# PEER experts on 192 tokens densely and on the last 64 by their chosen rows

## The chip, the cores and the metric

The kernel runs on one core of a Trainium2 chip. The metric is the device time of one execution in microseconds (us): 3215.98 us, the median of three runs (3214.02 to 3218.95). The profile below is of one execution of the same program, with a span of 3216.2 us from its first to its last instruction.

## The reference

Two transformer blocks act on 256 tokens of width 2048, all in float32. What matters here is the last part of the first block, a "PEER" layer with 16384 experts:

```python
def peer(h, w_q, sub_keys, expert_u, expert_v):        # T = 256 tokens, D = 2048
    q = (xt @ w_q).reshape(T, 8, 2, 128)
    s = jnp.einsum('thpd,hpnd->thpn', q, sub_keys)     # 8 heads x 2 halves x 128 keys
    s_half, i_half = lax.top_k(s, 16)
    ...                                                # best 16 of the 16 x 16 pairs of each head
    g = jax.nn.softmax(top_s, axis=-1)                 # 8 x 16 = 128 chosen experts for a token
    u = expert_u[ic]                                   # expert_u, expert_v: 16384 x 2048
    a = jnp.einsum('cd,ced->ce', xc, u)
    w = gc * jax.nn.gelu(a)
    return jnp.einsum('ce,ced->cd', w, expert_v[ic])
```

Each token needs 128 of the 16384 rows of `expert_u` and of `expert_v`. The first block's attention comes before it; the second block (`w_in_2`, two branches, `w_out_2`, and a feed-forward with `w_up` and `w_down`) comes after it.

## The kernel before

**Weights in pieces.** All big weights are cut on the host into pieces of 128 x 1024 float32 (512 KB). The list `order` fixes the order of its 1104 pieces: among them 32 of `peer_w_q`, 256 of `peer_u`, 256 of `peer_v`, then 160 of `w_in_2`. SyncE loads piece after piece into `raw` (`NR` = 5 buffers). ScalarE rounds it to fp32r (`split_hi`, into `whi`, `NH` = 3 buffers), VectorE subtracts to get the remainder (`split_lo`, into `wlo`), and TensorE multiplies high part by high, high by low and low by high. That makes two kinds of products:

- `gemm` (`peer_v`, `w_in_2`, `w_down`): the activations are the stationary operand, the weights move, 12 matmuls of 512 columns for a piece (`gemm_piece`).
- `gemm_wide` (`peer_w_q`, `peer_u`, `w_up`): the weights are stationary; high and low activations of 256 tokens stand side by side and move together, so a piece takes 8 matmuls of 512 columns with `whi` and 8 of 256 columns with `wlo` (`wide_piece`). Four pieces make one unit of 256 output rows.

**The PEER layer is dense.** `peer_u` is multiplied with all tokens (64 units of 256 experts). `u_post` adds the two halves of the result on VectorE (`gelu_sum`, 128 x 512), scales it (`gelu_scale`), takes the gelu on ScalarE and stores it to `scr_a`. Meanwhile `routing` finds each token's 128 experts on VectorE, and GpSimd writes their gates into a zeroed table `scr_g` of 16384 x 256 in DRAM with 256 indirect DMAs (`gate_scatter`, 128 elements of 4 bytes each, L2913). `fetch` reads gelu and gate back, `prepare` multiplies them and splits the product, and `peer_v` is multiplied with it. `add_residual` adds each of its products to `R`.

**What sets the order.** The whole program is recorded by one walk of Python generators (`walk`); `tasks` holds those that run beside the products, and `step()` moves each of them to its next `yield`. `gemm_wide` calls `step()` after three of a unit's four pieces, and more steps are taken where it must have a result. So a generator's number of yields fixes beside which piece each of its instructions stands. Every engine then runs its own list in that order and waits on semaphores: a VectorE instruction that waits for a DMA holds up the `split_lo` behind it. `scatter` issues four indirect DMAs for each `yield`.

## Time and profile before

| | |
|---|---|
| runs | 3214.02, 3215.98, 3218.95 us |
| span of the profiled execution | 3216.2 us |
| TensorE busy | 3182.5 us, 99% |
| VectorE busy | 2082.1 us, 65% |
| ScalarE busy | 1523.1 us, 47% |
| GpSimd busy | 531.3 us, 17% |
| moved by DMA | 663.12 MB, mean 206 GB/s |

The span is the time to compare with a run; no time around it is listed. "Idle before" in a group is the time in which the engine stood still just before these instructions, with what it waited for. A stretch's DMA share is the mean busy share of the core's 16 DMA engines. A matmul's shown duration overlaps the next one's, so a matmul's cost is read from the distance of starts.

### The profile page before, as it was taken

The page shows a single profiled execution, that of the slowest core. Times are in us where ns is not written, and L with a number is a line of the kernel's source. Part 1 is how long each engine was busy: PE and PEld are TensorE (multiplying, and loading weights), DVE is VectorE, ACT ScalarE, POOL GpSimd, SP SyncE. Part 2 cuts the span into 40 slices and gives each one's busy share as a digit, 9 for nine tenths or more (in the row PEclk, how much of TensorE's full clock was granted, in tenths as well). Part 3 has the DMA queues.
Part 4 walks back from the last instruction along what each step waited for, and adds up shares of the span by engine and source line. Part 5 has one row for each costly group of instructions (what it writes and reads, how often), then busy time and mean ns, then how long its engine had stood idle before and what let it go on. Part 6 is the DMA issues. An engine that isn't in the chain of part 4 may idle for free.

```text
span 3216.2 us, 41890 instructions
## 1 busy us (share of the span) xinstructions
PE 3182.5 (99%) x16120; PEld 2701.5 (84%) x16120; DVE 2082.1 (65%) x3024; ACT 1523.1 (47%) x2006; POOL 531.3 (17%) x326
## 2 busy tenths in 40 slices
PE   9899999999999999999999999999999999999998
PEld 7788888888888888888888888888888888888886
DVE  6786588886555576666666665555465755555556
ACT  5655454454444444444444544455444544444443
POOL 0010007788777400000000000000000000000000
PEclk9999999999999999999999999999999999999999
DMA  7466558888888876677776555455655655666654
GB/s 260 138 231 240 185 206 208 211 215 216 213 208 213 266 278 232 235 241 248 247 244 195 189 189 176 163 171 171 202 198 175 198 193 186 195 190 190 191 192 147
DMA packets 220599, 663.12 MB, mean 206 GB/s; under 512 B 56896, under 2 KB 56912, under 8 KB 217584
## 3 DMA queue, kind: packets, MB, share of 16 engines
q1 hardware_dynamic: 170784, 600.81, 56.8%
q0 software_dynamic: 49472, 59.59, 8.8%
q8 instruction: 127, 2.08, 0.3%
q14 instruction: 72, 0.59, 0.1%
q10 hardware_dynamic: 144, 0.05, 0.0%
HBM read 624.57 MB, written 35.78 MB: 205 GB/s over the span
## 4 chain that ended last, share of the span: by engine, by line
PE 96%; DVE 2%; ACT 1%; issue 1%; DMA 0%; SPq 0%; DVEq 0%; ACTq 0%
PE PS L1785 94%; PE PS L1880 1%; DVE wlo L2285 0%; ACT whi L2041 0%; DMA raw<-in_w_in_a 0%; DVE AA L2339 0%; ACT M L2015 0%; DVE Y L2451 0%; ACT Y L2141 0%; DVE R L2814 0%; DVE BB L2339 0%; DVE M L2481 0%; DVE RT L2269 0%; DVE Y L2532 0%; DVE M L2391 0%
## 5 line engine op out<-in xcount | busy, mean ns | idle before, releaser
L2285 DVE TENSOR_TENSOR wlo<-raw,whi 128x1024 fp32r<-128x1024 f32 x1101 | 1342.5, 1223 | 737.3 <-ACT whi L2041 727.5
L2041 ACT ACTIVATE whi<-raw 128x1024 fp32r<-128x1024 f32 x1101 | 1159.9, 1058 | 1012.1 <-PE PS L1785 983.0
L1785 PE MATMUL PS<-whi,AA 128*128 128x512 f32 x2816 | 703.6, 391 | 3.4 <-DVE AA L2339 1.8
L1785 PE MATMUL PS<-whi,BB 128*128 128x512 f32 x2640 | 666.7, 393 | 1.7 <-DVE wlo L2285 1.2
L1785 PEld LDWEIGHTS PS<-whi,AA 128*128 128x128 f32 x2816 | 525.1, 188 | 113.3 <-DVE AA L2339 2.2
L1785 PE MATMUL PS<-BB,whi 128*128 128x512 f32 x2304 | 577.4, 392 | 0.5 <-DVE BB L2339 0.5
L1785 PEld LDWEIGHTS PS<-whi,BB 128*128 128x128 f32 x2640 | 491.3, 188 | 102.2 <-DVE wlo L2285 1.6
L2913 POOL DMA_INDIRECT scr_g<-M x256 | 480.1, 1875 | 352.0 <-DVE M L2687 224.5
L1785 PEld LDWEIGHTS PS<-BB,whi 128*128 128x128 f32 x2304 | 414.4, 189 | 74.9 <-DVE BB L2339 0.8
L1785 PE MATMUL PS<-wlo,AA 128*128 128x512 f32 x1408 | 379.1, 389 | 0.0
L1785 PE MATMUL PS<-wlo,BB 128*128 128x512 f32 x1320 | 356.4, 390 | 0.5 <-DVE wlo L2285 0.5
L1785 PEld LDWEIGHTS PS<-BB,wlo 128*128 128x128 f32 x2304 | 314.3, 190 | 22.5
L1785 PE MATMUL PS<-BB,wlo 128*128 128x256 f32 x2304 | 321.2, 282 | 0.0
L1785 PEld LDWEIGHTS PS<-wlo,AA 128*128 128x128 f32 x1408 | 264.3, 188 | 55.5
L1785 PEld LDWEIGHTS PS<-wlo,BB 128*128 128x128 f32 x1320 | 247.7, 188 | 53.1 <-DVE wlo L2285 0.9
L1785 PE MATMUL PS<-AA,whi 128*128 128x512 f32 (+1 forms) x1056 | 262.1, 389 | 1.8 <-DVE AA L2380 1.1
L1785 PEld LDWEIGHTS PS<-AA,whi 128*128 128x128 f32 (+1 forms) x1056 | 188.5, 187 | 35.6 <-DVE AA L2380 1.4
L1785 PEld LDWEIGHTS PS<-AA,wlo 128*128 128x128 f32 (+1 forms) x1040 | 141.7, 189 | 10.3 <-DVE wlo L2285 0.4
L1785 PE MATMUL PS<-AA,wlo 128*128 128x256 f32 (+1 forms) x1040 | 147.3, 282 | 0.0
L2580 DVE TENSOR_TENSOR R<-R,PS 128x512 f32<-128x512 f32 x128 | 82.2, 684 | 77.1 <-PE PS L1785 77.1
L2941 POOL TENSOR_TENSOR R<-R,M 128x512 f32<-128x512 f32 x4 | 5.9, 1489 | 707.7 <-ACT M L2015 707.7
L2015 ACT ACTIVATE M<-TMP 128x512 f32<-128x512 f32 x64 | 40.5, 632 | 152.1 <-DVE TMP L2706 137.1
(252 smaller groups left out, 1520.5 us busy)
## 6 DMA issues: line engine op xcount, KB each, us to landing
raw<-in_peer_u SPq DMA_DIRECT2D x256, 512.0 KB
raw<-in_peer_v SPq DMA_DIRECT2D x256, 512.0 KB
raw<-in_w_in SPq DMA_DIRECT2D x160, 512.0 KB
raw<-in_w_up SPq DMA_DIRECT2D x128, 512.0 KB
raw<-in_w_down SPq DMA_DIRECT2D x128, 512.0 KB
raw<-in_w_out SPq DMA_DIRECT2D x64, 512.0 KB
raw<-in_w_in_a SPq DMA_DIRECT2D x32, 512.0 KB
scr_g<-M POOLq DMA_DIRECT2D x8, 2048.0 KB, 32.5
```

The lines of the kernel that those rows point to most:

```text
L1785: return e.matmul(outp, l, r, start=start, stop=stop)
L1880: last = e.transpose(banks[bank][:, 128 * n:128 * n + 128], s, ident)
L2015: e.activation(o, x, func, **kw).then_inc(sem(name), 1)
L2041: e.activation(whi[:, n % NH, :], raw[:, n % NR, :], ACT.Copy).then_inc(s_hi, 1)
L2285: e.tensor_tensor(wlo[:, n % NH, :], raw[:, n % NR, :], bf(whi[:, n % NH, :]), ALU.subtract).then_inc(s_lo, 1)
L2580: last = e.tensor_tensor(R[:, t, c], R[:, t, c], b[t][:, :], ALU.add)
L2913: e.indirect_dma_start(out=D["scr_g"].rearrange("e (t o) -> (e t) o", o=1), out_offset=bass.IndirectOffsetOnAxis(ap=EID[t][:, k:k + 1], ax ...
L2941: e.tensor_tensor(R[:, t, c], R[:, t, c], scaled[j], ALU.add).then_inc(sem("pool_added"), 1)
```

## The change

The constant `NSP` = 64 parts the tokens: the first `TD` = 192 keep the dense form, the last 64 get their experts by rows.

- Dense part: `peer_u` runs with `T=TD`, so a piece takes 8 matmuls of 384 columns and 8 of 192. `peer_v` is cut as `peer_u` is and uses `gemm_wide` with `T=TD` in place of `gemm`; its result comes out transposed and is added to `YT`, a transposed copy of the rows, which is turned back at the end. The two activation buffers `AA` and `BB` change roles from there on.
- The table `scr_g` has 192 columns; the 128 scatters of the second token tile write 64 elements each. `scatter` issues 1.5 for each `yield`, the second tile is routed first, and `fetch` and `prepare` work by 256 experts instead of 1024.
- Sparse part: 128 partitions hold 64 tokens twice, and each of the two copies takes 64 of a token's 128 experts. For each m in 0..63 GpSimd gathers 128 rows of `peer_u` (8 KB each, 1 MB in all, L3177) and VectorE multiplies and sums them with the token's row (`sparse_dot`, two halves of 1024). After the gelu and the gate, for each m GpSimd gathers 128 rows of `peer_v` (L3184), and VectorE adds them weighted (`sparse_add`, two halves). A matmul with the constant `select` sums the two copies.
- At u = 59 the recording takes steps with no product between them until the last dot is recorded.

The core of the diff:

```diff
+NSP = 64
+TD = 256 - NSP
...
+    SCATTERS, DOT_PACE, ADD_PACE = 1.5, ((1, 1), (1, 0)), (1, 1)
...
                     for k in range(16):
+                        while credit < 1.0:
+                            yield
+                            credit += SCATTERS
+                        credit -= 1.0
                         go("gate_scatter", t, 16 * h + k, fresh("POOL", ready, landed[t] if k == 0 else None))
                         mark = landing(f"gate_scattered{t}")
-                        if k % 4 == 3:
-                            yield
...
-                    for t in range(2):
+                    for t in (1, 0):
...
+            def sparse_dots():
+                dots, rows_free = {}, {}
+                for m in range(NSP + 2):
+                    if m < NSP:
+                        while not t_z:
+                            yield
+                        go("gather_u", m, fresh("POOL", sp_routed[0], sp_routed[1], t_z, rows_free.get(m - 3)))
+                        dots[m] = landing(f"rows_landed{m % 3}")
+                    for half in range(2):
+                        for _ in range(DOT_PACE[m % 2][half]):
+                            yield
+                        if m >= 2:
+                            go("sparse_dot", m - 2, half, fresh("DVE", dots[m - 2], t_z))
+                            last = up("DVE", "sparse_step")
+                    if m >= 2:
+                        rows_free[m - 2] = last
...
             for u in range(64):
-                gemm_wide("peer_u", [u], BB, nP, u_post)
+                gemm_wide("peer_u", [u], BB, nP, u_post, T=TD)
...
+                if u == 59:
+                    while not sp_weighed or len(g_written) < 2:
+                        step()
+                    assert not idle
+                    for n in range(4):
+                        fetch(n)
+                if u == 61:
+                    tasks.append(prepare())
...
+            def sparse_adds():
+                rows_in, rows_free = {}, {}
+                for m in range(NSP + 1):
+                    if m < NSP:
+                        go("gather_v", m, fresh("POOL", sp_weighed, bar, g_written, rows_free.get(m - 2)))
+                        rows_in[m] = landing(f"rows_landed{m % 2}")
+                    for half in range(2):
+                        for _ in range(ADD_PACE[half]):
+                            yield
+                        if m >= 1:
+                            go("sparse_add", m - 1, half, fresh("DVE", rows_in[m - 1], sp_weighed, bar, latest["DVE"]))
+                            last = up("DVE", "sparse_step")
...
+            for c in range(8):
...
+                for db in range(8):
+                    gemm_wide("peer_v", [8 * c + db], HB[c % 2], wB[c], v_post, T=TD)
...
-                    x = both[:, kt, :, :].rearrange("p a n -> p (a n)")
+                    x = both[:, kt, :, 0:T]
...
-                        last = mm(b[m][:, 0:256], wlo[:, s, w], both[:, kt, 0, :], False, kt == 15)
+                        last = mm(b[m][:, 0:T], wlo[:, s, w], both[:, kt, 0, 0:T], False, kt == 15)
...
+            def sparse_dot(m, half, ready):
...
+                e.tensor_tensor_reduce(out=x, in0=x, in1=z_all[:, c], scale=1.0, scalar=0.0, op0=ALU.mult, op1=ALU.add,
+                                       accum_out=sp_dot[:, half, m:m + 1]).then_inc(sem("sparse_step"), 1)
...
+                    last = e.scalar_tensor_tensor(out=v_sum[:, c], in0=x, scalar=sp_w[:, m:m + 1], in1=v_sum[:, c],
+                                                  op0=ALU.mult, op1=ALU.add)
...
+                n = (128, P0)[t]
                 e.indirect_dma_start(out=D["scr_g"].rearrange("e (t o) -> (e t) o", o=1),
...
+            def gather_u(m, ready):
...
+                e.indirect_dma_start(out=u_rows[m % 3], out_offset=None, in_=D["peer_u_rows"],
+                                     in_offset=bass.IndirectOffsetOnAxis(ap=sp_id[:, m:m + 1], axis=0)
+                                     ).then_inc(sem(f"rows_landed{m % 3}"), 16)
```

How it moves the instructions, at three places.

**GpSimd, from the routing's end to the first fetch.** Before, the last scatters stand alone (L2913), and the fetches follow (L2922 gelu, L2923 gates):

```order
L2913 DMA scr_g<-M 4194304x1 [waits gate_scattered1]
L2913 DMA scr_g<-M 4194304x1 x15
L2922 DMA M<-scr_a 128x2048 [waits gelu_stored2,gelu_stored1,gelu_stored3,gelu_stored0,gate_scattered0,gelu,gate_scattered1,piece_used,gelu_scaled]
L2923 DMA M<-scr_g 128x8x256
L2922 DMA M<-scr_a 128x2048 [waits gelu_stored2,gelu_stored3,gelu_stored1,gelu_stored0]
L2923 DMA M<-scr_g 128x8x256
```

Now, after 112 of the 256 scatters (L3150), the second norm's gain (L3158), the tokens' rows (L3164) and then the gathers of `peer_u` (L3177) stand between them:

```order
L3158 DMA M<-in_gain 64x2048 [waits gelu,piece_used,gelu_scaled]
L3150 DMA scr_g<-M 3145728x1 [waits gate_scattered0]
L3150 DMA scr_g<-M 3145728x1 x7
L3164 DMA M<-M 64x2048 [waits sparse_step]
L3164 DMA M<-M 64x2048
L3177 DMA M<-in_peer_u_rows,PTb 128x2048 [waits z_landed,routes_landed1,routes_landed0]
L3150 DMA scr_g<-M 3145728x1 x3
L3177 DMA M<-in_peer_u_rows,PTb 128x2048
L3150 DMA scr_g<-M 3145728x1
L3177 DMA M<-in_peer_u_rows,PTb 128x2048
L3150 DMA scr_g<-M 3145728x1 x3
L3177 DMA M<-in_peer_u_rows,PTb 128x2048 [waits sparse_step]
```

From the first gather on, 136 scatters and 64 gathers share this engine's list, about two scatters for a gather; before, nothing stood between two scatters.

**VectorE, beside `peer_u`.** Before, behind the routing (its last instruction is the CAST), an added half (L2700) and a scaling (L2706) stand between the splits (L2285) of every four pieces:

```order
L2687 CAST M<-M 128x64 [waits vector_step]
L2285 TENSOR_TENSOR wlo<-raw,whi 128x1024 [waits piece_used,hi_split]
L2706 TENSOR_TENSOR TMP<-TMP,PTb 128x512 [waits gelu_sum]
L2285 TENSOR_TENSOR wlo<-raw,whi 128x1024 [waits piece_used,hi_split] x2
L2700 TENSOR_TENSOR TMP<-TMP,PS 128x512 [waits gelu_low]
L2285 TENSOR_TENSOR wlo<-raw,whi 128x1024 [waits piece_used,hi_split] x2
```

Now dots (L2911, each with a read of its sum, `PTb 128x1`) stand there too, four for every four pieces, each second one behind a gather's `rows_landed`; here where the last dots begin:

```order
L2911 ISA M,PTb<-M 128x1024 [waits rows_landed2]
L2911 ISA PTb 128x1
L2464 TENSOR_TENSOR wlo<-raw,whi 128x1024 [waits piece_used,hi_split]
L2879 TENSOR_TENSOR TMP<-TMP,PS 128x384 [waits gelu_low]
L2911 ISA M,PTb<-M 128x1024
L2911 ISA PTb 128x1
L2911 ISA M,PTb<-M 128x1024 [waits rows_landed0]
L2911 ISA PTb 128x1
L2911 ISA M,PTb<-M 128x1024
L2911 ISA PTb 128x1
L2885 TENSOR_TENSOR TMP<-TMP,PTb 128x384 [waits gelu_sum]
L2911 ISA M,PTb<-M 128x1024 [waits rows_landed1]
```

101 of the 128 dots have a split each between them; the last 27 follow one another with no split (L2464) between, up to the weights of the sparse part.

**VectorE, beside `peer_v`.** Before, two residual additions (L2580) for every four pieces, and the gate products (L2715) now and then:

```order
L2580 TENSOR_TENSOR R<-R,PS 128x512 [waits piece_used]
L2580 TENSOR_TENSOR R<-R,PS 128x512
L2285 TENSOR_TENSOR wlo<-raw,whi 128x1024 [waits piece_used,hi_split]
L2715 TENSOR_TENSOR M<-M 128x256 [waits gate_fetched0,gelu_fetched0]
L2715 TENSOR_TENSOR M<-M 128x256
L2285 TENSOR_TENSOR wlo<-raw,whi 128x1024 [waits piece_used,hi_split]
```

Now for every four pieces three weighted additions (L2932) and two additions to `YT` (L2947, L2949), with the gate products and remainders (L2891, L2897) between:

```order
L2932 SCALAR_TENSOR_TENSOR M<-M,PTb 128x1024 [waits lo_split]
L2464 TENSOR_TENSOR wlo<-raw,whi 128x1024 [waits piece_used,hi_split]
L2891 TENSOR_TENSOR M<-M 128x384 [waits gate_fetched2]
L2897 TENSOR_TENSOR AA<-M,AA 128x2x192 [waits expert_hi]
L2932 SCALAR_TENSOR_TENSOR M<-M,PTb 128x1024 [waits expert_lo,rows_landed1]
L2464 TENSOR_TENSOR wlo<-raw,whi 128x1024 [waits piece_used,hi_split]
L2932 SCALAR_TENSOR_TENSOR M<-M,PTb 128x1024 [waits lo_split]
L2464 TENSOR_TENSOR wlo<-raw,whi 128x1024 [waits piece_used,hi_split]
L2947 TENSOR_TENSOR Y<-Y,PS 128x2x192 [waits piece_used]
L2949 TENSOR_TENSOR Y<-Y,PS 128x2x192 [waits vector_step]
L2464 TENSOR_TENSOR wlo<-raw,whi 128x1024 [waits piece_used,hi_split]
```

The 128 weighted additions stand beside the first 172 of the 256 pieces.

## Rows read from the trace of the kernel before

**Rows 1.** The page: busy time and share of each engine, and the chain's engines
```profile
PE 3182.5 (99%) x16120; PEld 2701.5 (84%) x16120; DVE 2082.1 (65%) x3024; ACT 1523.1 (47%) x2006; POOL 531.3 (17%) x326
...
PE 96%; DVE 2%; ACT 1%; issue 1%; DMA 0%; SPq 0%; DVEq 0%; ACTq 0%
```

**Rows 2.** Busy time in stretches (columns in the first line)
```profile
core 0: us, PE busy (x) PEld busy (x) DVE busy (x) ACT busy (x) POOL busy (x), PEclk, DMA share, GB/s
411.00:1128.00 717.00, 717.00 (x4124) 631.53 (x4123) 507.80 (x815) 349.21 (x402) 483.08 (x260) 1.00 0.83 217
485.00:750.00 265.00, 265.00 (x1519) 233.17 (x1518) 231.31 (x489) 131.62 (x152) 210.16 (x113) 1.00 0.86 213
...
1128.00:1827.00 699.00, 699.00 (x3094) 578.34 (x3094) 469.80 (x578) 313.85 (x340) 20.11 (x28) 1.00 0.70 236
...
200.00:240.00 40.00, 39.67 (x235) 34.53 (x234) 32.31 (x119) 24.69 (x75) 4.51 (x4) 1.00 1.02 392
```

**Rows 3.** ScalarE's first copies of finished peer_u units (ns min/median/max, first and last start)
```profile
L2015 ACT ACTIVATE TMP<-PS x4: 597/598/599, 420.6 to 457.7; 128x512 f32<-128x512 f32 x4
```

**Rows 4.** TensorE in order of time in peer_u (start us, us, what, count)
```profile
700.56 2.00 PE L1785 MATMUL PS<-BB,whi 128*128 128x512 f32 x8
702.40 1.12 PE L1785 MATMUL PS<-BB,wlo 128*128 128x256 f32 x8
703.35 2.00 PE L1785 MATMUL PS<-BB,whi 128*128 128x512 f32 x8
```

**Rows 5.** The same in peer_v
```profile
1500.00 1.07 PE L1785 MATMUL PS<-wlo,AA 128*128 128x512 f32 x4
...
1502.72 1.07 PE L1785 MATMUL PS<-wlo,AA 128*128 128x512 f32 x4
```

**Rows 6.** The same in the attention scores, 128 and 256 columns
```profile
162.98 0.86 PE L1785 MATMUL PS<-BB,AA 128*128 128x128 f32 x6
163.69 0.23 PE L1785 MATMUL PS<-M 128*128 128x128 bf16 x1
...
164.57 0.96 PE L1785 MATMUL PS<-BB,AA 128*128 128x256 f32 x6
165.37 0.23 PE L1785 MATMUL PS<-M 128*128 128x128 bf16 x1
```

**Rows 7.** VectorE's groups by form (count, busy us, mean ns, idle before)
```profile
L2285 DVE TENSOR_TENSOR wlo<-raw,whi 128x1024 fp32r<-128x1024 f32 x1101 | 1342.5, 1223 | 737.3 <-ACT whi L2041 727.5 <-PE PS L1785 3.8 <-issue 3.8
...
L2715 DVE TENSOR_TENSOR M<-M 128x256 f32<-128x256 f32 x128 | 48.3, 418 | 0.0
...
L2706 DVE TENSOR_TENSOR TMP<-TMP,PTb 128x512 f32<-128x512 f32 x64 | 43.8, 685 | 0.0
...
L2814 DVE SCALAR_TENSOR_TENSOR R<-Y,ST,R 128x512 f32<-128x512 f32 x11 | 7.9, 749 | 0.1
...
L2299 DVE CUSTOM_DVE_ANT_0 Y<-R 128x512 f32<-128x512 f32 x4 | 2.7, 684 | 0.0
...
L2299 DVE DVE_READ_ACCUMULATOR2_ANT ST<- 128x1 f32 x4 | 0.3, 82 | 0.0
```

**Rows 8.** GpSimd's groups by form
```profile
L2913 POOL DMA_INDIRECT scr_g<-M x256 | 480.1, 1875 | 352.0 <-DVE M L2687 224.5 <-issue 86.2 <-DMA scr_g<-M 41.3
...
L2922 POOL DMA_DIRECT2D M<-scr_a x16 | 8.7, 544 | 554.6 <-DVE AA L2722 507.1 <-issue 42.9 <-DMA scr_g<-M 4.6
```

**Rows 9.** GpSimd in order of time at the end of the scatters
```profile
1085.09 2.58 POOL L2913 DMA_INDIRECT scr_g<-M  x1 [0.30 <-issue]
...
1090.01 2.57 POOL L2913 DMA_INDIRECT scr_g<-M  x1 [0.30 <-issue]
1097.19 0.60 POOL L2922 DMA_DIRECT2D M<-scr_a  x1 [4.62 <-DMA scr_g<-M]
```

**Rows 10.** DMA issues (KB each, median us to landing)
```profile
M<-scr_a POOLq DMA_DIRECT2D x16, 1024.0 KB, 7.2
```

More of the change, by code:

```diff
@@ new lines, in walk, with fetch, prepare @@
+            lt, vdone, tw_free = {}, {}, {}
+            def fetch(n):
+                w = bar if n < 4 else tw_free[n - 4]
+                go("fetch", n, fresh("POOL", w, a_written[n], g_written, sp_weighed))
+                lt[n] = [landing(f"gate_fetched{n % 4}"), landing(f"gate_fetched{n % 4}")]
+            def prepare():
+                gated, high = {}, {}
+                for n in range(66):
+                    free = None
+                    for k, what in ((n, "gate"), (n - 1, "hi"), (n - 2, "lo")):
+                        if not 0 <= k < 64:
+                            continue
+                        free = bar if k < 8 else peer_read if k < 16 else vdone[k // 8 - 2]
+                        if what == "gate":
+                            go("expert_gate", k, fresh("DVE", lt[k]))
+                            gated[k] = up("DVE", "expert_gate")
+                        elif what == "hi":
+                            go("expert_hi", k, fresh("ACT", gated[k], free, bar))
+                            high[k] = up("ACT", "expert_hi")
+                        else:
+                            go("expert_lo", k, fresh("DVE", high[k], free))
+                            wB[k // 8].append(up("DVE", "expert_lo"))
+                            tw_free[k] = [wB[k // 8][-1]]
+                            if k + 4 < 64:
+                                fetch(k + 4)
+                    yield
+                    yield
+                    while n + 1 < 64 and (n + 1) // 8 >= 1 and (n + 1) // 8 > v_at[0] + 1:
+                        yield
@@ new lines, in rows_turned @@
+            def rows_turned():
+                for k0 in range(0, 16, 2):
+                    bank, bfree = yield from wait_for(misc)
+                    tk = transposed([R[:, t, 128 * (k0 + i):128 * (k0 + i) + 128] for i in range(2) for t in range(2)],
+                                    bank, t_R, bfree)
+                    yield
+                    go("rows_turned_in", bank, k0, fresh("ACT", tk, bar))
+                    turned_in.append(up("ACT", "rows_turned"))
+                    misc.give(bank, turned_in[-1])
+                    yield
@@ L1301, in walk @@
+            wB, v_at, turned_in = {c: [] for c in range(8)}, [-1], []
+            peer_read = []
             for u in range(64):
-                gemm_wide("peer_u", [u], BB, nP, u_post)
+                gemm_wide("peer_u", [u], BB, nP, u_post, T=TD)
                 if u == 1:
@@ L1337, in walk @@
+            for c in range(8):
+                v_at[0] = c
+                if c == 7:
+                    while not sp_added:
+                        step()
+                for db in range(8):
+                    gemm_wide("peer_v", [8 * c + db], HB[c % 2], wB[c], v_post, T=TD)
+            tasks.append(row_stat())
             everything = everyone()
@@ L1835, in gemm_rows, with wide_piece @@
                     last.then_inc(sem("rows_done"), 1)
-            def wide_piece(i, b, c, both, high, low, free, second):
+            def wide_piece(i, b, c, both, T, high, low, free, second):
                 s = i % NH
@@ L1973, in sub_scores, with sparse_turn @@
                 last.then_inc(s_used if end else sem("sub_scores"), 1)
+            def sparse_turn(bank, k0, kn, ready):
+                for mark in ready:
+                    e.wait_ge(*mark)
+                for k in range(kn):
+                    w = slice(128 * (k0 + k), 128 * (k0 + k) + 128)
+                    last = mm(banks[bank][:, NSP * k:NSP * k + NSP], v_sum[:, w], select, True, True)
+                last.then_inc(sem("transposed"), 1)
             def da_scores(bank, h, t, ready):
@@ new lines, in sparse_sum, with sparse_gate, sparse_add @@
+            def sparse_sum(ready):
+                for mark in ready:
+                    e.wait_ge(*mark)
+                e.tensor_tensor(sp_dot[:, 0, :], sp_dot[:, 0, :], sp_dot[:, 1, :], ALU.add).then_inc(sem("sparse_step"), 1)
+            def sparse_gate(ready):
+                for mark in ready:
+                    e.wait_ge(*mark)
+                e.tensor_tensor(sp_w, sp_w, sp_gate, ALU.mult).then_inc(sem("sparse_step"), 1)
+            def sparse_add(m, half, ready):
+                for mark in ready:
+                    e.wait_ge(*mark)
+                c = slice(1024 * half, 1024 * half + 1024)
+                x = v_rows[m % 2][:, c]
+                if m == 0:
+                    last = e.tensor_scalar(v_sum[:, c], x, sp_w[:, 0:1], None, ALU.mult)
+                else:
+                    last = e.scalar_tensor_tensor(out=v_sum[:, c], in0=x, scalar=sp_w[:, m:m + 1], in1=v_sum[:, c],
+                                                  op0=ALU.mult, op1=ALU.add)
+                last.then_inc(sem("sparse_step"), 1)
@@ L3085 @@
     A["peer_u"] = cut_u(I["peer_u"][0].T)
-    A["peer_v"] = cut_down(I["peer_v"][0])
+    v = I["peer_v"][0]
+    A["peer_v"] = np.concatenate([cut_u(v[k:k + 2048]) for k in range(0, 16384, 2048)])
+    A["peer_u_rows"] = I["peer_u"][0]
+    A["peer_v_rows"] = v
+    A["gain2"] = I["norm2_gain"][0]
     w = I["w_in_2"][0]
```

346 lines of the change are left out of this document (232 added, 114 removed).

## The prediction

> **What bounds the kernel now.** I read the page's busy times and the chain of waits first: TensorE is busy 99% of the span and holds 96% of the chain [rows 1]. So before the change only TensorE's own time counts, and everything else hides behind it. The reader is to see next how much of that cover each stretch has left. Then I read the busy times in stretches: between 411 and 1128 us (`peer_u`) VectorE works 508 of 717 us and GpSimd 483; in the routing part (485 to 750) VectorE works 231 of 265 us, 87%, and beside `peer_v` 470 of 699 [rows 2]. So the cover is thin where the change makes TensorE faster.
>
> `peer_u` starts at about 409 us: the first of its units is copied at 420.6 [rows 3], and a unit of four pieces takes 4 x 2.79. `peer_v` starts at 1128 and ends at 1827 [rows 2].
>
> **The change part by part.**
>
> *TensorE.* In `peer_u` the eight high matmuls begin 1.84 us before the eight low ones (230 ns each), and these 0.95 us before the next piece (119 ns each): 2.79 us a piece [rows 4]. In `peer_v` a piece takes 1502.72 - 1500.00 = 2.72 us [rows 5]. For 384 columns I take the middle between 256 and 512: (119 + 230) / 2 = 174 ns. For 192 columns the nearest rows are six fp32r matmuls of 128 columns in 0.71 us (118 ns) and six of 256 in 0.80 us (133 ns) beside each other [rows 6]: halving the columns gives 11%. So 192 columns get little; 115 ns is my value, between 105 (119 x 118 / 133) and 119. New piece: 8 x 0.174 + 8 x 0.115 = 2.31 us. If TensorE stayed the bound this would save 256 x 0.48 = 123 us in `peer_u` and 256 x 0.41 = 105 us in `peer_v`.
>
> *VectorE beside `peer_u`.* A split costs 1.223 us. An instruction of 384 columns lies halfway between 418 ns (256) and 685 ns (512): 0.55 us. A dot is not in the trace at this width; the nearest row is the multiply-and-sum of 512 columns with 684 ns, plus the step from 512 to 1024 of a plain operation (1223 - 685 = 538), plus the read of 82 ns: 1.30 us [rows 7]. It could be 1.37 (684 x 2) at most by that row and not below 1.22.
>  - Up to the first dot stand 142 pieces, most beside routing. VectorE's 231 us in 265 are 0.873 x 2.79 = 2.44 us a piece, less 2 x 0.135 / 4 for the narrower sums: 2.37. I take 2.39: 142 x 2.39 = 339 us where it was 396. The first dot stands at 409 + 339 = 748 us.
>  - Then 101 dots for 101 pieces: 1.223 + 0.55 x 2 / 4 + 1.30 = 2.80 us a piece, 283 us, and 27 dots with no piece beside them, 35 us. TensorE waits during these: it has at most the pieces already split.
>
> *GpSimd.* This list decides, in my reading. A scatter takes 1.875 us on average [rows 8] and 0.30 until the next [rows 9]: 2.175. Before, 256 of them hid in 717 us. Now 136 scatters are left when the first gather is issued, for the list holds the gain's load back until routing is done, and 64 gathers stand between them. A gather has no row. From below, a plain load of 1 MB takes 0.54 us of GpSimd [rows 8]; from above nothing in the trace is dearer than 2.58 [rows 9]. It takes its 128 row numbers from a column as the scatter does, so I take the scatter's 2.175. Sum: 200 x 2.175 = 435 us. 48 of the 136 move 64 elements instead of 128; half of what they cost over a plain load would save 48 x 0.67 = 32 us, nothing would save 0, and I take 16. At the start of a round a scatter waits for the last round to land; 4.62 us is what the last wait took [rows 9], and nine rounds are left, most behind a round of the other tile: 10 us. So the last gather is issued at 748 + 435 - 16 + 10 = 1177 us. Bounds for this term: 136 x 1.5 + 64 x 0.85 = 258 us to 136 x 2.4 + 64 x 2.9 = 512 us, where 429 is taken. VectorE's own 318 us lie beside it and under it.
>    Behind the waiting dots stand VectorE's splits, so TensorE waits with them; this is how a GpSimd list becomes the kernel's bound.
>  - Then the last gather lands (7.2 us as a plain 1 MB load does [rows 10]), two dots, the sum, gelu and gate: 13 us. 14 pieces are left, 14 x 2.31 + 3 for the restart = 35 us, and the first fetches hide in it. `peer_v` starts at 1177 + 13 + 35 = 1225, 97 us later than at 1128.
>
> *Beside `peer_v`.* 172 pieces share VectorE with 128 weighted additions. The nearest row for one is 749 ns for 512 columns [rows 7], so 0.749 + 0.538 = 1.29 us. With two additions to `YT` for four pieces and 94 gate products and remainders: (172 x 1.223 + 128 x 1.29 + 180 x 0.55) = 474 us, 2.76 a piece, more than TensorE's 2.31 and more than the 2.72 of before. The other 84 pieces need 1.77 us of VectorE each and go by TensorE: 194 us. Sum 668. Each gather of `peer_v` has only two buffers: it is issued when the additions two before it are done, three steps or about 11 us ahead of its use, and needs 2.2 us of GpSimd and 7.2 to land; some will be late. I add 15 us (bounds 0 and 64 x 2 = 128): 683 instead of 699, 16 us gained.
>  In bytes, the 172 pieces, 64 gathers and the fetches beside them (172 x 0.524 + 67 + 18 = 176 MB) need 449 us at the 392 GB/s that the queues reached between 200 and 240 us [rows 2]: just below 474, so the transfers are no bound by this row, but near one.
>  The Trainium skill (page "DMA: Bandwidth & Descriptors", section "Where 436 GB/s comes from") has loads from HBM bound by about 358 GB/s a core. The trace disagrees, since 392 were reached for 40 us; by the page the same bytes would take 491 us, and this stage 17 us longer.
>
> *Ends.* The 64 transposes of the rows are there before and after. Sixteen small matmuls and the turning back stand behind covered steps: 3 us. ScalarE has 47% [rows 1] and gets less to do. What this costs if its cover goes is not more than those few us.
>
> Sum, against the profiled execution's span, which lies on the median of the runs: 3216 + 97 - 16 + 3 = 3300 us.
>
> **The rivals.**
>  - A, VectorE alone sets the pace beside `peer_u`, GpSimd keeps up. For it: the plain load's 0.54 us shows that many descriptors can be cheap, and half-size scatters may be cheaper. Against it: the scatter's 1.875 us. `peer_v` would start at 748 + 283 + 35 + 11 + 35 = 1112 (16 earlier), and with no late gather its stage takes 668 (31 less): 3216 - 16 - 31 + 3 = 3172. This is the faster side. It decides if a scatter and a half per dot stay under VectorE's time: two scatters and a gather within 5.6 us instead of 6.5.
>  - B, TensorE stays the bound throughout: 3216 - 123 - 105 = 2988. VectorE's sums speak against it in three of four stretches.
>  - C, fp32r matmuls of 192 columns lose their rate (165 ns instead of 115: two cycles a column). For it: halving 256 columns gave only 11% [rows 6]. Against: 118 ns for 128 columns leaves room for one cycle a column and a floor beside it. A piece takes 2.71 us: 142 x 0.32 + 14 x 0.4 + 84 x 0.4 = 85 us more, 3385.
>  - D, gathers of `peer_v` late by 2 us each: 3300 + 113 = 3413. Two buffers and 11 us of lead against 9.4 speak for it, the landing in a fuller queue too; against it, that the load's 7.2 us are already from a busy queue.
>
> **How the numbers follow.** My forecast, GpSimd's list as the bound, 0.60 (its own range 3230 to 3365); A 0.17, B 0.03, C 0.09, D 0.11. The likeliest gives 3300 us. The range that holds 8 in 10 reaches from A to just short of D: 3165 to 3400. A measurement of this kernel tells about 0.2% (6 us) from no change. Faster: A, B and a tail of the first, 0.22; within 0.2%: 0.03; slower: 0.75.
>
> **What would show it.** Right: TensorE's busy share falls in `peer_u` after routing; VectorE waits there for the gathers (L2911 behind DMA `peer_u_rows`) and GpSimd is near 100% busy from about 485 us to the last gather near 1177; a gap of tens of us in TensorE before the last 14 pieces of `peer_u`; high and low matmuls begin 174 and 115 ns apart; beside `peer_v` VectorE is above 90% until two thirds of the stage, then TensorE is full again. Wrong: the gathers take far less than 2 us of GpSimd, or scatters of 64 elements do; the first `peer_v` matmul stands before 1128; or low matmuls of 192 columns take 160 ns.

## The result

The changed kernel takes 3301.4 us (median of 4 runs, 3296.9 to 3304.1) against 3217.3 us for the kernel before: ratio 1.0263, 95% interval 1.0249 to 1.0278. It is 2.6% slower; the forecast was 3300 us. The profiled execution has a span of 3295.0 us.

Boundaries, read from the first matmul on each stage's operands (us):

| | before | forecast | after |
|---|---|---|---|
| first dot | | 748 | 765.0 |
| last gather of `peer_u` issued | | 1177 | 1172.1 |
| `peer_v` starts | 1127.9 | 1225 | 1217.9 |
| `peer_v` stage lasts | 699.1 | 683 | 688.5 |

The whole loss is beside `peer_u` (+90), and `peer_v` gives 11 back. Both are read from the profiled executions, whose spans differ by 79 us (3295.0 and 3216.2); the medians differ by 84. The page after, busy times and chain; they answer to [rows 1].

```profile
PE 3037.0 (92%) x17208; PEld 2726.5 (83%) x17208; DVE 2325.6 (71%) x3349; ACT 1494.7 (45%) x2039; POOL 787.7 (24%) x557
...
PE 62%; DVE 13%; POOL 11%; issue 6%; DMA 5%; ACT 2%; SPq 0%; DVEq 0%; ACTq 0%; POOLq 0%
```

TensorE held 96% of the chain and holds 62%; VectorE, GpSimd, its issue gaps and transfers have come in. A share of 24% says nothing against GpSimd as a bound: its work lies in one part of the span. The stretches after, for [rows 2]:

```profile
core 0: us, PE busy (x) PEld busy (x) DVE busy (x) ACT busy (x) POOL busy (x), PEclk, DMA share, GB/s
411.00:485.00 74.00, 71.97 (x505) 71.29 (x505) 66.45 (x132) 40.93 (x51) 9.04 (x7) 1.00 0.74 224
485.00:755.00 270.00, 255.60 (x1727) 247.95 (x1727) 244.99 (x496) 137.98 (x173) 214.81 (x121) 1.00 0.87 234
755.00:1100.00 345.00, 262.58 (x1564) 256.03 (x1564) 247.56 (x338) 115.89 (x148) 289.72 (x163) 0.88 0.95 316
1100.00:1180.00 80.00, 17.32 (x118) 16.91 (x116) 43.08 (x70) 8.64 (x14) 59.31 (x38) 0.61 0.78 238
...
1320.00:1670.00 350.00, 313.90 (x2038) 298.43 (x2036) 330.93 (x352) 147.69 (x159) 121.25 (x112) 0.96 0.98 371
1670.00:1906.00 236.00, 229.91 (x1601) 229.05 (x1600) 176.09 (x204) 124.03 (x164) 20.94 (x31) 0.99 0.80 256
```

Until 755 us TensorE keeps 95%. Then it waits a quarter of the time, and from 1100 to 1180 it works 17 us of 80. From 755 to 1100 GpSimd is busy 290 us and stands for about 0.3 us before each of its 163 instructions, so hardly anything is free there. Beside `peer_v` VectorE is at 95% until 1670 us, and the transfers at 0.98.

The groups of the added work (count, busy us, mean ns, idle before), for [rows 7, 8]:

```profile
L3150 POOL DMA_INDIRECT scr_g<-M x256 | 478.5, 1869 | 90.2 <-issue 77.1 <-DMA scr_g<-M 13.1
...
L2932 DVE SCALAR_TENSOR_TENSOR M<-M,PTb 128x1024 f32<-128x1024 f32 x126 | 161.9, 1285 | 21.1 <-DMA M<-in_peer_v_rows,PTb 13.9
L2911 DVE CUSTOM_DVE_ANT_0 M<-M 128x1024 f32<-128x1024 f32 x128 | 153.5, 1221 | 95.5 <-DMA M<-in_peer_u_rows,PTb 95.4
...
L3184 POOL DMA_INDIRECT M<-in_peer_v_rows,PTb x64 | 104.7, 1636 | 243.2 <-DVE M L2932 234.0 <-DVE M L2930 5.0 <-issue 4.2
...
L3177 POOL DMA_INDIRECT M<-in_peer_u_rows,PTb x64 | 90.1, 1408 | 29.1 <-issue 18.3 <-DMA M<-M 7.4 <-DVE PTb L2911 3.4
```

In `peer_u` the dots wait for landed rows (95.4 us) and the gathers hardly for dots (3.4 us). In `peer_v` it is the other way round: gathers wait 234 us for sums, sums 13.9 us for rows. The direction of such a pair of waits tells which side is short.

TensorE in order of time at the end of `peer_u`:

```profile
1116.80 1.03 PE L1928 MATMUL PS<-BB,wlo 128*128 128x192 f32 x8
1183.74 2.93 PE L1928 MATMUL PS<-BB,whi 128*128 128x384 f32 x8 [65.91 <-ACT whi L2192]
1186.47 1.79 PE L1928 MATMUL PS<-BB,wlo 128*128 128x192 f32 x8
...
1190.37 1.59 PE L1928 MATMUL PS<-BB,whi 128*128 128x384 f32 x8
1191.79 1.03 PE L1928 MATMUL PS<-BB,wlo 128*128 128x192 f32 x8
1192.66 1.59 PE L1928 MATMUL PS<-BB,whi 128*128 128x384 f32 x8
```

The first two rows are the hole: 65.9 us without a matmul, since the order of unit 59 puts all dots that are left ahead of the next splits. The last three give the new piece: 1.42 us for eight high matmuls (178 ns each), 0.87 us for eight low ones (109 ns), 2.29 in all.

### The profile page after: what moved, and what is told of

It is laid out like the page before. It is cut to its first block, busy times and chain, and to the rows that moved or that the text cites. A ratio compares the mean times of both kernels' runs of the same rounds, so it can differ in the third digit from the quotient of the medians.

```text
span 3295.0 us, 44692 instructions
## 1 busy us (share of the span) xinstructions
PE 3037.0 (92%) x17208; PEld 2726.5 (83%) x17208; DVE 2325.6 (71%) x3349; ACT 1494.7 (45%) x2039; POOL 787.7 (24%) x557
## 4 chain that ended last, share of the span: by engine, by line
PE 62%; DVE 13%; POOL 11%; issue 6%; DMA 5%; ACT 2%; SPq 0%; DVEq 0%; ACTq 0%; POOLq 0%
PE PS L1928 61%; POOL scr_g L3150 8%; DVE wlo L2464 7%; DMA M<-in_peer_v_rows,PTb 4%; POOL M L3177 3%; PE PS L2023 1%; ACT whi L2192 1%; DVE M L2891 0%; DVE M L2787 0%; DVE M L2932 0%; DVE M L2791 0%; DVE TMP L2885 0%; DVE TMP L2879 0%; DVE BB L2897 0%; DVE Y L2947 0%
## 5 line engine op out<-in xcount | busy, mean ns | idle before, releaser
L2464 DVE TENSOR_TENSOR wlo<-raw,whi 128x1024 fp32r<-128x1024 f32 x1101 | 1340.8, 1222 | 578.5 <-ACT whi L2192 573.7
L1928 PE MATMUL PS<-BB,whi 128*128 128x384 f32 (+1 forms) x4352 | 961.2, 364 | 156.1 <-ACT whi L2192 138.6
L1928 PEld LDWEIGHTS PS<-BB,whi 128*128 128x128 f32 x4352 | 775.3, 195 | 205.5 <-issue 78.8
L1928 PEld LDWEIGHTS PS<-BB,wlo 128*128 128x128 f32 x4352 | 585.5, 196 | 62.8 <-DVE wlo L2464 49.8
L1928 PE MATMUL PS<-BB,wlo 128*128 128x192 f32 (+1 forms) x4352 | 597.3, 281 | 34.1 <-DVE wlo L2464 33.7
L3150 POOL DMA_INDIRECT scr_g<-M x256 | 478.5, 1869 | 90.2 <-issue 77.1
L1928 PE MATMUL PS<-AA,whi 128*128 128x384 f32 (+1 forms) x1056 | 217.5, 347 | 23.4 <-DVE AA L2897 23.4
L2911 DVE CUSTOM_DVE_ANT_0 M<-M 128x1024 f32<-128x1024 f32 x128 | 153.5, 1221 | 95.5 <-DMA M<-in_peer_u_rows,PTb 95.4
L2932 DVE SCALAR_TENSOR_TENSOR M<-M,PTb 128x1024 f32<-128x1024 f32 x126 | 161.9, 1285 | 21.1 <-DMA M<-in_peer_v_rows,PTb 13.9
L3184 POOL DMA_INDIRECT M<-in_peer_v_rows,PTb x64 | 104.7, 1636 | 243.2 <-DVE M L2932 234.0
L1928 PE MATMUL PS<-AA,wlo 128*128 128x192 f32 (+1 forms) x1040 | 145.3, 281 | 10.7 <-DVE wlo L2464 10.7
L3177 POOL DMA_INDIRECT M<-in_peer_u_rows,PTb x64 | 90.1, 1408 | 29.1 <-issue 18.3
```

What stands on the lines that cost most here:

```text
L1928: return e.matmul(outp, l, r, start=start, stop=stop)
L2464: e.tensor_tensor(wlo[:, n % NH, :], raw[:, n % NR, :], bf(whi[:, n % NH, :]), ALU.subtract).then_inc(s_lo, 1)
L2911: e.tensor_tensor_reduce(out=x, in0=x, in1=z_all[:, c], scale=1.0, scalar=0.0, op0=ALU.mult, op1=ALU.add, accum_out=sp_dot[:, half, m:m + ...
L2932: last = e.scalar_tensor_tensor(out=v_sum[:, c], in0=x, scalar=sp_w[:, m:m + 1], in1=v_sum[:, c], op0=ALU.mult, op1=ALU.add)
L3150: e.indirect_dma_start(out=D["scr_g"].rearrange("e (t o) -> (e t) o", o=1), out_offset=bass.IndirectOffsetOnAxis(ap=EID[t][0:n, k:k + 1], ...
L3177: e.indirect_dma_start(out=u_rows[m % 3], out_offset=None, in_=D["peer_u_rows"], in_offset=bass.IndirectOffsetOnAxis(ap=sp_id[:, m:m + 1], ...
```

## The experiments

Twelve kernels. The totals are medians of the runs, the boundaries come from the one profiled execution of each (us):

| kernel | total | `peer_v` starts | stage | longest wait of TensorE before it |
|---|---|---|---|---|
| after | 3301.4 | 1217.9 | 688.5 | 65.9 |
| e1 packed | 3270.3 | 1183.0 | 689.3 | 44.4 |
| e2 no second scatter | 3254.5 | 1171.7 | 692.3 | 43.8 |
| e3 thin dots | 3218.6 | 1176.7 | 651.4 | 59.0 |
| e4 thin, short rows | 3162.6 | 1160.0 | 612.1 | 54.9 |
| e5 few rows | 3077.6 | 1072.0 | 615.5 | 30.9 |
| e6 32 tokens | 3232.6 | 1135.6 | 702.0 | 12.1 |
| e7 dense, stationary | 3256.4 | 1127.1 | 734.9 | |
| e8 32 tokens, packed | 3236.5 | 1146.5 | 701.4 | 11.7 |
| e9 short rows | 3276.5 | 1208.6 | 677.4 | 64.5 |
| e10 short rows, packed | 3240.2 | 1173.6 | 676.2 | 29.4 |
| e11 32, packed, spread | 3204.4 | 1136.6 | 672.4 | 4.7 |
| e12 32, sums spread | 3198.5 | 1135.6 | 672.8 | 7.0 |

e2 to e5, e9 and e10 leave work out, and each of them ran once. The differences read from them are of 9 us or more. The five runs of e1 lie within 8.5 us of each other, so a single difference of 9 us stands little above the spread.

One unit of `peer_u` (four pieces) has 4 dots, 2 gathers and, as long as scatters are left, 4.5 scatters beside it. The time of two gathers is therefore the time of a unit. In the changed kernel 30 units from the first gather on take 411 us, 13.7 each.

### e1: a quarter of the scatters off GpSimd's list

```diff
-                    for k in range(16):
+                    for k in range(16 if t == 0 else 8):
...
+            def pack_rows(g, ready):
...
+                both = M[0:64, 10496:10752].rearrange("p (a h s j) -> p a h s j", a=2, h=8, s=2)
+                for s in range(2):
+                    for a in range(2):
+                        e.dma_start(packed[64 * s:64 * s + 64, a, 4 * g:4 * g + 4, :],
+                                    both[:, a, 4 * g:4 * g + 4, s, :]).then_inc(sem(f"routes_landed{g}"), 16)
```

> The gate chosen for tokens 128 to 191 are first copied so that 128 partitions hold them (8 of a head's 16 choices each), which takes 64 of the 256 scatters off GpSimd's list and adds 8 small transfers; nothing else changes. Theory (GpSimd's list sets the pace of the peer_u products after the routing): 64 x about 2.17 us = 139 us less on the list, so the last gather goes out near 1040 instead of 1172 us and VectorE becomes the bound behind it; the peer_v stage starts 80 to 130 us earlier than at 1218, the kernel takes 3175 to 3225 us. Rival A (VectorE's load alone sets the pace) and the DMA rival (the queues are full, 0.97 busy share): under 20 us gained, 3280 to 3300 us. Peer_v stage unchanged at 688 us by every theory.

Measured: 3270.3 us, ratio to before 1.0163 (1.0149 to 1.0177). The start came 35 us earlier, where I had expected 80 to 130 and the rivals under 20. So GpSimd's list was a bound, and taking 64 scatters off it is worth 35 us. But e1 takes them off the list's end: the scatters that are left still stand 4.5 to a unit beside the first 17 units, which take 230 us, 13.5 each. What bounds the kernel where they are gone is read under e2. What GpSimd waited for between 755 and 1120 us, after and in e1:

```profile
POOL scr_g L3150 <- issue: 36.0, 118, 0.3
POOL M L3177 <- issue: 15.8, 52, 0.3
POOL M L3177 <- DMA M<-M: 7.4, 1, 7.4
POOL scr_g L3150 <- DMA scr_g<-M: 5.3, 1, 5.3
```
```profile
POOL M L3192 <- DVE PTb L2917: 94.6, 25, 9.5
POOL scr_g L3156 <- issue: 23.4, 77, 0.3
POOL M L3192 <- issue: 10.1, 33, 0.3
```

After, GpSimd waits for its own issue, once for the tokens' rows to be spread over both copies and once for a round of scatters to land; in e1 it waits 95 us for dots to free a buffer.

### e2: half of the scatters away

```diff
-                    for k in range(16):
+                    for k in range(16 if t == 0 else 0):
```

> Leaves out all 128 scatters of tokens 128 to 191 (their gates stay zero). Theory: GpSimd is then no bound at all, what is left is VectorE's load: peer_v starts at 1070 to 1110 us, total 3150 to 3190 us (my rival A gave 3172). If GpSimd was not the bound: no change, 3300 us. If it gives no more than the packed kernel, VectorE has taken over in both.

Measured: start 1171.7, 11 us before e1, though another 64 scatters are gone. My rival A put VectorE's own load at a start of 1112. The stretch from 755 to 1120 us in e2:

```profile
755.00:1120.00 365.00, 274.82 (x1670) 269.56 (x1669) 278.61 (x390) 124.42 (x161) 183.59 (x118) 0.86 0.96 339
```

VectorE is at 76%, GpSimd at 50%, TensorE at 75%, and only the queues look full (0.96). But this is an average over two parts. Up to 933 us 56 scatters are left, and 13 units take 179 us, 13.8 each, 15 us of it waits of GpSimd for landings. From 944 us on come eleven units of 11.7 us each. Ten of them, and what the engines wait for in them:

```profile
952.00:1069.00 117.00, 100.60 (x636) 99.20 (x635) 101.63 (x141) 47.43 (x60) 27.03 (x21) 0.93 0.99 376
```
```profile
DVE wlo L2465 <- ACT whi L2193: 15.4, 10, 1.5
ACT M L2167 <- DVE TMP L2886: 67.5, 10, 7.0
PE PS L1929 <- ACT whi L2193: 16.4, 10, 2.3
```

VectorE works 10.2 us of a unit's 11.7 and waits 1.5, once, for ScalarE's rounded copy. ScalarE has that copy in its list behind the gelu of the unit, and the gelu waits 6.8 us a unit for the scaling that VectorE does behind the dots. So VectorE's work and this exchange between two in-order lists set the pace: 2.92 us a piece. e1 has seven units of the same 11.7 us once its scatters are gone, and so has e10, where the queues have a share of only 0.67:

```profile
1015.00:1073.00 58.00, 49.72 (x319) 49.03 (x318) 50.32 (x71) 23.55 (x30) 13.19 (x10) 0.94 0.67 209
```

### e3: dots and sums over 64 of 1024 columns

```diff
-                c = slice(1024 * half, 1024 * half + 1024)
+                c = slice(1024 * half, 1024 * half + 64)
                 x = u_rows[m % 3][:, c]
...
-                c = slice(1024 * half, 1024 * half + 1024)
+                c = slice(1024 * half, 1024 * half + (1024 if m == 0 else 64))
                 x = v_rows[m % 2][:, c]
```

> Every dot and every sum of sparse rows works on 64 of its 1024 columns (the rest is left out); gathers, waits and counts stay. Beside peer_u, theory (GpSimd's list): start of peer_v stays within 15 us of 1218. Rival A (VectorE): 100 us or more earlier. Beside peer_v, theory (VectorE's load): the stage falls from 688 to about 600 us, TensorE's own 591 us or the transfers' 226 MB at 371 GB/s = 610 us. If the transfers of the gathered rows set the pace there: stays above 660 us.

Measured: start 1176.7, 41 us earlier, between the two expectations. The reason is in GpSimd's rows: the same 256 scatters became shorter.

```profile
L3150 POOL DMA_INDIRECT scr_g<-M x256 | 442.9, 1730 | 91.6 <-issue 76.5 <-DMA scr_g<-M 14.8 <-DVE M L2867 0.3
```

The 136 scatters from the first gather on took 224.7 us for 258.9, and the 64 gathers 78.9 for 90.1: 45 us, enough for all of the gain. So the list was the bound here, and what VectorE does beside an indirect transfer changes its length (the last section has the rows). Stage of `peer_v`: 651.4 us, and there the transfers are full. From 1350 to 1600 us:

```profile
1350.00:1600.00 250.00, 237.16 (x1597) 232.36 (x1596) 186.84 (x276) 117.06 (x126) 87.57 (x86) 0.99 1.02 405
```

### e4: the same, and 0.5 KB of each row

```diff
-                e.indirect_dma_start(out=u_rows[m % 3], out_offset=None, in_=D["peer_u_rows"],
+                e.indirect_dma_start(out=u_rows[m % 3][:, 0:128], out_offset=None,
+                                     in_=D["peer_u_rows"].rearrange("e (a c) -> (e a) c", c=128),
```
(and the same for the gathers of `peer_v` but the first)

> As the kernel with thin dots and sums, and each gather fetches 128 columns of its rows (0.5 KB for 8 KB), same number of indirect transfers. Beside peer_u: if GpSimd's list counts by instruction, peer_v still starts within 15 us of the thin kernel; if bytes in the queues set the pace, 50 us or more earlier. Beside peer_v: 591 us (TensorE alone) against the thin kernel's figure; the difference is what 64 MB of rows cost.

Measured: start 1160.0, 17 us before e3, near the "within 15"; stage 612.1, 39 us shorter, which is what the rows' 64 MB cost once VectorE has room. From 1350 to 1600 TensorE is full at last:

```profile
1350.00:1600.00 250.00, 250.00 (x1753) 250.00 (x1753) 203.07 (x291) 125.77 (x135) 83.05 (x90) 1.00 0.84 281
```

### e5: the dense half alone (2 of 64 gathers left)

```diff
-                for m in range(NSP + 2):
-                    if m < NSP:
+                for m in range(NM + 2):
+                    if m < NM:
```
(with NM = 2, in the sums too)

> Only 2 of the 64 gathers, dots and sums of each table are left (62 left out); all 256 scatters and the 192-column products stay. It shows the dense half of the change alone. My terms: TensorE 2.31 us a piece, VectorE 2.39 us a piece beside peer_u, so peer_v starts at 1050 to 1085 us (411 + 256 x 2.39 = 1023, and the burst before the last pieces), and the peer_v stage takes 587 to 605 us; total 3030 to 3065 us. Rival C (192-column products lose rate): stage of 640 us or more. If the 256 scatters alone held GpSimd as the bound, peer_v would start later than 1100 us.

Measured: 3077.6 us, start 1072.0, stage 615.5: the start as expected, the stage 10 us and the total 13 us above what I expected. In the middle of the stage 32 pieces take 73.4 us, 2.29 each, as forecast (2.31); rival C is out. Of the 28 us that the stage lasts over 8 x 73.4 = 587, 25 are in its first part, 98.8 us for 32 pieces. Even here the last of the 256 scatters is issued at 1050.6, the fetches wait for it, and TensorE stands still for 30.9 us before the last pieces. TensorE alone would come to about 407 + 256 x 2.29 = 993 (an estimate from its first `peer_u` matmul at 406.7 us), so that wait is the largest part of the 79 us above it, though not all: TensorE's other waits from 411 us on make 23 us.

### e6: 32 tokens by rows

```diff
-NSP = 64
+NSP = 32
```

> NSP = 32: the last 32 tokens by rows (32 gathers of 128 rows a table, half of the dots and sums), dense products on 224 tokens. If GpSimd's list sets the pace beside peer_u: 32 x 1.75 = 56 us less on it, peer_v starts at 1140 to 1165 us; if bytes and VectorE set it, nearer 1110 us. TensorE needs an estimated 2.55 to 2.65 us a piece (448 and 224 columns, between the rows for 192 and for 256), so the peer_v stage becomes TensorE's: 655 to 685 us. Total 3180 to 3240 us: about the kernel before. If the 64-token form is only near its optimum by size, this one would lie between before and after, near 3260.

Measured: 3232.6 us, 1.0049 (1.0035 to 1.0062). Start 1135.6, 82 us before the 64-token form: more than the list's 56 us, and 4 us earlier than the range I expected. The stage got longer, 702 us, where I had expected 655 to 685.

### e7: the new `peer_v` layout, all 256 tokens dense

```diff
-TD = 256 - NSP
+TD = 256
...
-            tasks.append(sparse_dots())
...
-            tasks.append(sparse_adds())
```

> The other half of the change by itself: peer_v weights stationary with all 256 tokens dense, no rows gathered, nothing left out. A piece then moves 512 columns 8 times and 256 columns 8 times; the rows of before for those shapes give 8 x 0.227 + 8 x 0.115 to 8 x 0.165 = 2.7 to 3.1 us. Theory: the layout is worth nothing by itself, peer_v stage 690 to 730 us and peer_v start within 15 us of before's 1128; total 3205 to 3255 us. If the layout is what costs the 84 us, total above 3280 us.

Measured: 3256.4 us, 1.0124 (1.0109 to 1.0140); start 1127.1 as before, stage 734.9, 5 us above what I expected, and the total 1 us above. The layout by itself costs 36 us: a piece takes 89.4 / 32 = 2.79 us for 2.72, which is 18 us, and the first 32 pieces take 106.1 us for 89.4. In that first part TensorE waits for the remainders of the first group (L2896):

```profile
L1927 PE MATMUL PS<-AA,whi 128*128 128x512 f32 x256 | 67.1, 403 | 12.3 <-DVE AA L2896 12.3
```

### e8: 32 tokens, scatters packed

```diff
-NSP = 64
+NSP = 32
...
-                    for k in range(16):
+                    for k in range(16 if t == 0 else 12):
```
(and 16 small copies, 12 of 16 choices in place and 4 onto the free 32 partitions)

> NSP = 32 and the choices of the 96 dense tokens of the second tile copied onto 128 partitions, 12 scatters a head for 16: 224 scatters in all, 16 small transfers more. If GpSimd's list still sets the pace beside peer_u at 32 tokens: 32 x 2.2 = 70 us less on it, less 12 us of copies, peer_v starts 30 to 60 us before that of the unpacked 32-token kernel (TensorE and VectorE allow about 1090 us); total 3130 to 3190 us, faster than both kernels. If by then VectorE or the transfers set it: less than 10 us gained.

Measured: 3236.5 us, no gain over e6 (3232.6). The scatters that packing takes away stood behind the last gather: from first to last gather it is 212 us here and 210 in e6, and behind that GpSimd costs TensorE only the one wait of 12.1 us in e6. The 16 copies put the first gather from 763.5 to 785.0 us, and between 755 and 1050 TensorE works 239 us:

```profile
755.00:1050.00 295.00, 238.68 (x1374) 222.54 (x1373) 201.77 (x260) 105.95 (x130) 240.44 (x137) 0.91 0.91 288
1050.00:1146.00 96.00, 96.00 (x620) 91.36 (x619) 57.33 (x59) 51.06 (x65) 30.56 (x24) 1.00 0.82 245
```

### e9 and e10: full dots and sums, short rows

The gathers of e4 beside the full dots and sums: e9 is otherwise the changed kernel, e10 is e1.

```diff
-                e.indirect_dma_start(out=u_rows[m % 3], out_offset=None, in_=D["peer_u_rows"],
+                if m < 3:
...
+                e.indirect_dma_start(out=u_rows[m % 3][:, 0:128], out_offset=None,
+                                     in_=D["peer_u_rows"].rearrange("e (a c) -> (e a) c", c=128),
```
(and the same for the gathers of `peer_v` from the third on)

> All 256 scatters, 128 gathers, dots and sums over 1024 columns stay, but each gather (from the fourth of peer_u and the third of peer_v on) fetches only the first 128 columns; the rest of a row is stale. Takes away only the bytes. Beside peer_u: if GpSimd's list is what is shortest there, peer_v starts within 15 us of 1218; if the transfers' bytes are, 40 us or more earlier. Beside peer_v: VectorE's load by my terms is 474 + 194 = 668 us, so the stage falls from 688 to about 670; if the bytes are the bound, to 612 to 625 (TensorE's figure).

> The packed kernel (192 scatters) with the same short rows. The packed kernel started peer_v at 1183 and left GpSimd half idle, VectorE at 76% and the DMA queues at 0.97. If the bytes are the bound behind GpSimd's list, peer_v starts at 1100 to 1140 us here; if VectorE's load (with its waits for landings) is, within 15 us of 1183. Peer_v stage as in the kernel with short rows alone.

Measured: beside `peer_u` the bytes matter little. Without them `peer_v` starts 9 us earlier with the full list and with the packed one. From first to last gather it is 11 us less (405 for 416) and 16 less (357 for 373); the first gather came 5 and 10 us later in these executions. A unit without scatters takes 11.7 us with and without the bytes, so the queues' 0.96 in e2 was no bound there. The bytes count in the last dots, which have no pieces beside them: the hole at unit 59 is 44 us in e1 and 29 in e10, and 27 dots at 1.14 us are 31. Besides the hole, TensorE in e10 has 25 short waits from 755 us on, 76 us in all. Beside `peer_v` the stage is 677 us in both. From 1350 to 1600 in e9 VectorE is at 97% and the transfers at 0.77:

```profile
1350.00:1600.00 250.00, 227.61 (x1492) 216.13 (x1491) 241.73 (x256) 108.46 (x117) 90.02 (x82) 0.97 0.77 242
```

### e11 and e12: the rows set apart

e11, on top of e8:

```diff
-    SCATTERS, DOT_PACE, ADD_PACE = 1.5, ((1, 1), (1, 0)), (1, 1)
+    SCATTERS, DOT_PACE, ADD_PACE = 1.5, ((2, 1), (1, 1)), (3, 2)
```

> The packed 32-token kernel with the same work set wider apart: a gather with its two dots every 2.5 scheduling steps for 1.5, and a gather with its two sums every 5 for 2, so that the rows arrive over most of each stage and not in its first part. In the packed 32-token kernel TensorE was busy 239 of 295 us between 755 and 1050, beside the gathers, and all of the time after the last gather. If the crowding of bytes and dots is the bound: peer_v starts at 1105 to 1125 us for 1146, its stage takes 675 to 690 us for 701, total 3185 to 3215 us, level with the kernel before or faster. If GpSimd's list of 224 scatters and 32 gathers is the bound whatever its order: no change, 3230 to 3240 us.

e12, on top of e6:

```diff
-    SCATTERS, DOT_PACE, ADD_PACE = 1.5, ((1, 1), (1, 0)), (1, 1)
+    SCATTERS, DOT_PACE, ADD_PACE = 1.5, ((1, 1), (1, 0)), (3, 2)
```

> The 32-token kernel with one thing altered: the sums of peer_v set apart (a gather with its two sums every 5 scheduling steps for 2); 256 scatters, and the dots as in the plain 32-token kernel. If the gain of the packed and spread kernel over the plain one (28 us) came from the sums alone: peer_v starts at 1130 to 1140 us as in the plain kernel (1135.6), its stage falls from 702 to 670 to 678 us, total 3195 to 3210 us, faster than the kernel before by 0.2 to 0.6%. If the packing of scatters or the spacing of the dots was needed for it: 3215 to 3235 us.

Measured: e11 3204.4 us, 0.9965 (0.9951 to 0.9978); e12 3198.5 us, 0.9949 (0.9936 to 0.9963). Both beat the kernel before, by 0.4% and 0.5%: small, but neither interval holds 1. Of the 34 us that e12 gains over e6, 29 are in the stage of `peer_v`, 672.8 us for 702.0, and the start is the same (1135.6), so the sums make the gain. With the sums apart TensorE is full from 1234 to 1639 us in e12:

```profile
1136.00:1234.00 98.00, 88.06 (x508) 81.22 (x507) 71.95 (x83) 41.23 (x48) 24.74 (x32) 0.90 0.86 306
1234.00:1639.00 405.00, 405.00 (x2567) 383.85 (x2566) 339.77 (x369) 189.42 (x201) 89.87 (x104) 1.00 0.89 316
```

Packing and spaced dots were not needed for it: in e11 they take short waits away from TensorE but start the dots 22 us later.

## Why the prediction was right, and where it was not

- **TensorE's piece.** 2.31 forecast, 2.29 measured (178 and 109 ns for 174 and 115). The layout was not priced: it takes 2.79 us a piece at 256 columns, not 2.72 (e7), and a slow first part. In the sum it stays unseen, since VectorE sets the stage.
- **First dot.** 748 forecast, 765.0 measured; the gather that feeds it was issued at 755.9 and took 9 us. The gain's load, the spread and the first landing were not in the step.
- **GpSimd's list.** 136 scatters and 64 gathers stand where forecast, and the last gather is 5 us off. The terms err against each other: a scatter took 258.9 / 136 = 1.90 us beside the dots, a gather 1.41 us where I took the scatter's 1.875, the half-size scatters saved nothing (1876 ns with 64 elements, 1862 with 128), and waits for landings cost 5 us, where I had 10. Measured from first to last gather: 258.9 + 90.1 + 68.1 in gaps and waits, 416 us for 429. That the last gather is only 5 us off is in part luck: the list began 8 us late and was 13 us short.
- **That this list decides.** Shown by e1 and e2, which shorten the list alone (35 and 46 us earlier), and by e3, where the same list ran faster. Where scatters are left a unit takes 13.7 us, and without them 11.7 (e1, e2): the list stands only 2.0 us a unit above the next bound.
- **VectorE beside the dots (rival A).** I had 2.80 us a piece once GpSimd keeps up; 2.92 were measured (e1, e2, e10). The terms err against each other again: VectorE's own work is 10.2 us a unit where I had 11.2, for dots and splits follow each other after 1.14 us, and the 1.5 us a unit for ScalarE's copy was not in the step. Which list item causes that wait is read from the traces; no kernel here moved the gelu or the scaling. The start of 1112 was not put to the test, since in e1 and e2 the scatters stand as densely as before beside the first 17 and 13 units. With the 13 units of e2 at 11.7 us as well, `peer_v` would start at about 1145 (an estimate: 1171.7 less 179 - 152). Most of the 33 us up to there are the first dot's 17 and half a microsecond in each of some 25 units.
- **The dots without a piece.** I counted 27 of them as 35 us. The hole that they leave in TensorE is 66 us after, where gathers still share the list with scatters, 44 in e1, where VectorE waits for landing rows (16 us of it from 1000 us on), and 29 in e10 with short rows.
- **Beside `peer_v`.** 668 us forecast for VectorE's load, 677 measured with the bytes away (e9); 15 us for late gathers, 11 measured (688.5 - 677.4). The price of lateness is the bytes': with VectorE free the full rows alone hold the stage at 651 us (e3), and both loads together give 688. I had held the transfers for no bound at 392 GB/s; 651 against TensorE's 612 (e4) says that they are one, 26 us behind VectorE.
   The queues moved 405 GB/s in e3 from 1350 to 1600 us. The Trainium skill (page "DMA: Bandwidth & Descriptors", section "Where 436 GB/s comes from") has about 358 GB/s from HBM for a core; this kernel on its one core went above it here, as it did in [rows 2].
- **Small terms.** `peer_u` starts at 406.7 us and not 409, and 13 pieces were left behind the last dots, not 14 (142 + 101 + 13 = 256): 2 us each.
- **Rivals.** B is out (e5 comes nearest, with the rows away), C is out (109 ns), D is out (13.9 us of waits for rows, not 128).

The 78.8 us between the two profiled executions split up. `peer_v`: layout +35.8 (e7 over before), 192 columns -119.4 (e5 over e7), rows +73.0 (after over e5), together -10.6. `peer_u`: layout -0.8, 192 columns -55.1 where TensorE's 123 us were on offer, for VectorE beside the routing and the last scatters hold e5 back; rows +145.9, together +90.0. The rest of the kernel: -0.6. The forecast had -16, +97 and +3. So each part is right within some us, but that the median lies 1.4 us from the forecast is luck.

## What to carry to other kernels

When the bound engine is relieved, price each helper's list in the stretch where the work lies, not over the span. And read how far behind the next one is: taking 64 scatters, about 139 us, off the bounding list gave 35. It matters where they are taken off, and an average over a stretch hides it: the stretch of e2 in which no engine was full held one part bound by GpSimd and one by VectorE with its wait for ScalarE. Added work on an in-order engine costs its waits too, so it belongs evenly beside the other work: setting the same sums apart made the stage 29 us shorter, where a shorter list was worth nothing at that size.
